# Hybrid trunk on one core: order of the second layer's input norms and first weights, low part of y on POOL, four banks for the q/k/v projection

## What is computed

```
for i in range(DEPTH):                       # 2 layers, x is (1, 512, 1024)
    hdn = rms_norm(x, norm_g[i])
    q, k, v, z (, f) = hdn @ w_in[i]         # 8 heads of 128, z a gate of the same width
    layer 0: q, k = rope(rms_norm(q)), rope(rms_norm(k)); y = causal block attention
    layer 1: q, k = rms_norm(q), rms_norm(k); y = attention with a bias from cumulated log f
    y = y * silu(z)
    x = x + y @ w_out[i]
```

## Time and profile before

| what | value |
| --- | --- |
| median of the runs | 556.06 us |
| the profiled execution | 555.65 us |
| its span, first to last instruction | 553.2 us |
| PE busy | 543.3 us, 98% |
| DVE busy | 408.5 us, 74% |
| POOL busy | 293.7 us, 53% |
| ACT busy | 286.9 us, 52% |
| granted TensorE clock, mean | 1.000 |

### The profile page before, as it was taken

How to read it: one execution, slowest core, us unless ns; L and a number is a source line. 1 busy time by engine, 2 the same in 40 slices (tenths; PEclk the granted TensorE clock), 3 DMA queues, 4 the chain that set the end, 5 groups by cost and what they waited for, 6 DMA issues and landing times.

```text
span 553.2 us, 9738 instructions
## 1 busy us (share of the span) xinstructions
PE 543.3 (98%) x2966; PEld 499.0 (90%) x2966; DVE 408.5 (74%) x1023; ACT 286.9 (52%) x841; POOL 293.7 (53%) x348
## 2 busy tenths in 40 slices
PE   6999999999999999999899999999999999999997
PEld 4999999999999999888688999999999999998887
DVE  3786899999999999974463767786868777779331
ACT  5746373737373737361445473837382837374400
POOL 5774545444444545451644486757565757476400
PEclk9999999999999999999999999999999999999999
DMA  9813313131313131222433336424241535132121
GB/s 259 244 22 111 103 54 100 55 98 57 95 57 95 57 95 57 95 78 73 108 95 78 96 80 95 99 74 105 67 118 53 118 53 133 53 118 70 45 95 58
DMA packets 78236, 49.94 MB, mean 90 GB/s; under 512 B 4089, under 2 KB 71417, under 8 KB 78210
## 3 DMA queue, kind: packets, MB, share of 16 engines
q1 hardware_dynamic: 78208, 49.61, 33.0%
q10 hardware_dynamic: 2, 0.00, 0.0%
HBM read 47.48 MB, written 2.11 MB: 90 GB/s over the span
## 4 chain that ended last, share of the span: by engine, by line
PE 50%; DVE 0%; issue 0%
PE banks L343 14%; PE banks L345 14%; PE banks L344 14%; PE banks L466 3%; PE banks L452 2%; PE banks L441 1%; PE banks L440 1%; PE banks L439 1%; PE banks L375 1%; PE banks L492 0%; PE banks L493 0%; DVE xs L948 0%; DVE xs L944 0%
## 5 line engine op out<-in xcount | busy, mean ns | idle before, releaser
L1079 POOL TENSOR_TENSOR w_lo<-w_raw,w_hi 128x512 fp32r<-128x512 f32 x147 | 190.1, 1306 | 82.9 <-ACT w_hi L602 82.9
L343 PE MATMUL banks<-w_hi,hT_hi 128*128 128x384 f32 x512 | 173.5, 339 | 2.6 <-DVE hT_lo L810 1.9
L344 PE MATMUL banks<-w_lo,hT_hi 128*128 128x384 f32 x512 | 171.6, 335 | 0.0
L345 PE MATMUL banks<-w_hi,hT_lo 128*128 128x384 f32 x512 | 171.6, 335 | 0.0
L867 DVE STREAM_TRANSPOSE banks<-qkn 32x256 f32<-32x256 f32 x240 | 109.4, 456 | 3.3
L343 PEld LDWEIGHTS banks<-w_hi,hT_hi 128*128 128x128 f32 x512 | 96.5, 188 | 4.5 <-POOL w_lo L1079 2.2
L344 PEld LDWEIGHTS banks<-w_lo,hT_hi 128*128 128x128 f32 x512 | 96.5, 188 | 0.6
L345 PEld LDWEIGHTS banks<-w_hi,hT_lo 128*128 128x128 f32 x512 | 96.4, 188 | 0.0
L602 ACT ACTIVATE w_hi<-w_raw 128x512 fp32r<-128x512 f32 x148 | 89.3, 638 | 13.5 <-DMA w_raw<-in_b_w_in_dram 13.4
L1095 POOL TENSOR_TENSOR msq<-ssq,eps 128x2 f32<-128x2 f32 x64 | 13.0, 203 | 127.1 <-ACT junk L638 127.1
L638 ACT ACTIVATE junk<-banks 128x128 bf16<-128x128 f32 x128 | 33.8, 271 | 48.8 <-PE banks L345 48.8
(11 more groups left out here) (110 smaller groups left out, 893.6 us busy)
## 6 DMA issues: line engine op xcount, KB each, us to landing
w_raw<-in_b_w_in_dram SPq DMA_DIRECT2D x64, 256.0 KB, 3.6
w_raw<-in_a_w_in_dram SPq DMA_DIRECT2D x52, 256.0 KB, 2.9
w_raw<-in_w_out_dram SPq DMA_DIRECT2D x32, 256.0 KB, 2.8
first_raw<-in_a_w_in_dram SPq DMA_DIRECT2D x12, 256.0 KB, 5.6
cos_t<-c_rows SPq DMA_DIRECT2D x8, 256.0 KB, 3.4
out_dram<-xs SPq DMA_DIRECT2D x7, 256.0 KB, 2.0
xs<-in_x_dram SPq DMA_DIRECT2D x3, 512.0 KB, 5.8
xs<-in_x_dram SPq DMA_DIRECT2D x2, 256.0 KB, 2.9
```

Source lines behind the costliest of these rows:

```text
L343: pe.matmul(dst, ah, bh, start=first and m == 0, stop=False)
L344: pe.matmul(dst, ah, bl, start=False, stop=False)
L345: mm = pe.matmul(dst, al, bh, start=False, stop=last and m == n - 1)
L1079: pool.tensor_tensor(w_lo[:, slot, k, :], raw, f32(w_hi[:, slot, k, :]), ALU.subtract).then_inc(wlo_set, by)
```

## The change

Four things. (1) The q/k/v projection of every head uses four banks, one for each tile (0, 1, 6, 7). The waits of PE (L393), ACT (L635) and POOL (L1094) that guard a reuse after two tiles now guard one after four, and the sums of squares and the reciprocal roots have four slots. The transposed q and k move to banks 4 and 5, which the transposed probabilities use as well, so that DVE's `turn_qk` gets one more wait, for the head's three low parts of probabilities. (2) In periods 1 to 6 of both layers the low part of y is made by POOL, between the reciprocal roots of tile 0 and the first weight chunk, and no longer by DVE ahead of the silu. (3) In the passage between the layers, on ACT the square of x tile t and the split of the transposed tile t - 1 stand ahead of the weight chunks 2t and 2t + 1 and no longer around them. (4) On POOL the reciprocal root of x tile t stands ahead of these two chunks.

```diff
-        ssq = sb("ssq", [P, 2, 2])
+        ssq = sb("ssq", [P, TILES, 2])
-        rstd = sb("rstd", [P, 2, 2])
+        rstd = sb("rstd", [P, TILES, 2])
-        Z_BANK, Y_BANK, QT_BANK, SPARE_BANK = 2, 3, 6, 6
+        Z_BANK, Y_BANK, QT_BANK, SPARE_BANK = 2, 3, 4, 6
         def qkv_bank(layer, h, t):
-            return (0, 1, 3, 4)[t] if layer == 0 and isinstance(h, int) and h == 0 else t % 2
+            return (0, 1, 3, 4)[t] if layer == 0 and isinstance(h, int) and h == 0 else (0, 1, 6, 7)[t]
         def turn_bank(layer, t):
-            return 3 if layer == 0 and t == 1 else QT_BANK
+            if layer == 1:
+                return QT_BANK
+            return 3 if t == 1 else SPARE_BANK
             def qkv(layer, h, slot, t):                       # PE
-                wait(pe, qkn_set, a - 1)
+                wait(pe, qkn_set, a - TILES + 1)
             def read_qkv(layer, h, s, t):                     # ACT
-                wait(act, rstd_set, a - 1)
+                wait(act, rstd_set, a - TILES + 1)
             def last(layer):                                  # ACT
                     for t in range(TILES):
-                        split_w(layer + 1, 0, 0, (2 * t, 2 * t + 1))
                         square_x(layer + 1, t)
                         if t >= 1:
                             split_hidden(layer + 1, t - 1)
+                        split_w(layer + 1, 0, 0, (2 * t, 2 * t + 1))
             def turn_qk(layer, h):                            # DVE
                 dve.wait_ge(qkn_set, TILES * (g + 1))
+                wait(dve, pTlo_set, 3 * g)
             def period(layer, h, s):                          # DVE
                 invert_sums(layer, h)
-                late_y(layer, h)
                 for n in range(4):
                     silu_part(layer, h, n)
             def last(layer):                                  # DVE
-                late_y(layer, h)
+                low_y(layer, h - 1)
             def rstd_qk(layer, h, t):                         # POOL
-                wait(pool, qkn_set, a - 1)
+                wait(pool, qkn_set, a - TILES + 1)
+            def low_y(layer, h):                              # POOL
+                g = HEADS * layer + h
+                pool.wait_ge(yhi_set, g + 1)
+                row = bass.ds(h, 1)
+                pool.tensor_tensor(yT_lo[:, row, :].rearrange("p a n -> p (a n)"), gz[:, 1, :],
+                                   f32(yT_hi[:, row, :].rearrange("p a n -> p (a n)")),
+                                   ALU.subtract).then_inc(ylo_set, 1)
             def period(layer, h, s):                          # POOL
                 rstd_qk(layer, h + 1, 0)
                 if layer == 1 and isinstance(h, int):
                     mask_bias(h)
+                if not isinstance(h, int):
+                    low_y(layer, h - 1)
                 split_w(layer, h + 2, s, (0,))
             def last(layer):                                  # POOL
                     for t in range(TILES):
+                        rstd_x(layer + 1, t)
                         split_w(layer + 1, 0, 0, (2 * t, 2 * t + 1))
-                        rstd_x(layer + 1, t)
```

More of the change, by code:

```diff
@@ L638, in read_qkv @@
                     sq = act.activation(junk[:, m, :], banks[:, qkv_bank(layer, h, t), m * P:(m + 1) * P],
-                                        ACT.Square, scale=SCALE, accum_out=ssq[:, t % 2, m:m + 1])
+                                        ACT.Square, scale=SCALE, accum_out=ssq[:, t, m:m + 1])
                 sq.then_inc(ssq_set, 1)
@@ L839, in norm_qk @@
                         last = dve.scalar_tensor_tensor(out=qkn[:, t, m, :], in0=banks[:, qkv_bank(layer, h, t), m * P:(m + 1) * P],
-                                                        scalar=rstd[:, t % 2, m:m + 1], in1=cos_t[:, 0, m, :],
+                                                        scalar=rstd[:, t, m:m + 1], in1=cos_t[:, 0, m, :],
                                                         op0=ALU.mult, op1=ALU.mult)
@@ L846, in norm_qk @@
                     dve.scalar_tensor_tensor(out=rot[:, t % 2, m].rearrange("p (a n) -> p a n", a=2), in0=swapped,
-                                             scalar=rstd[:, t % 2, m:m + 1],
+                                             scalar=rstd[:, t, m:m + 1],
                                              in1=sin_t[:, t, m].rearrange("p (a n) -> p a n", a=2),
@@ L852, in norm_qk @@
                     part = banks[:, qkv_bank(layer, h, t), m * P:(m + 1) * P]
-                    dve.scalar_tensor_tensor(out=part, in0=part, scalar=rstd[:, t % 2, m:m + 1], in1=cos_t[:, t, m],
+                    dve.scalar_tensor_tensor(out=part, in0=part, scalar=rstd[:, t, m:m + 1], in1=cos_t[:, t, m],
                                              op0=ALU.mult, op1=ALU.mult).then_inc(rot_set, 1)
@@ L1019, in begin @@
                 split_qk(layer, h)
-            def late_y(layer, h):
-                if not isinstance(h, int) or h > 0:
-                    low_y(layer, h - 1)
             def period(layer, h, s):
@@ L1093, in rstd_qk @@
                 pool.wait_ge(ssq_set, a + 1)
-                wait(pool, qkn_set, a - 1)
-                pool.tensor_tensor(msq[:, t % 2, :], ssq[:, t % 2, :], eps[:, :], ALU.add).then_inc(msq_set, 1)
+                wait(pool, qkn_set, a - TILES + 1)
+                pool.tensor_tensor(msq[:, t % 2, :], ssq[:, t, :], eps[:, :], ALU.add).then_inc(msq_set, 1)
                 pool.wait_ge(msq_set, a + 1)
-                pool.tensor_tensor(rstd[:, t % 2, :], msq[:, t % 2, :], power[:, :], ALU.pow).then_inc(rstd_set, 1)
+                pool.tensor_tensor(rstd[:, t, :], msq[:, t % 2, :], power[:, :], ALU.pow).then_inc(rstd_set, 1)
             pool.memset(one[:, :], 1.0).then_inc(ones_row, 1)
```

## The result

The changed kernel takes 563.4 us (median of 5 runs, 562.57 to 564.62) against 556.06; the ratio is 1.0134, with a 95% interval of 1.0119 to 1.015. That is slower, as forecast, by 7.3 us in place of 5.7, and the time lies 0.4 us above the upper end of the range. The profiled execution took 562.99 us; its span, 561.0, is 7.8 us longer than before.

What follows compares the result with a forecast made beforehand. PE, busy 98% of the span, was taken as the bound, with layer 0 paced by ACT, POOL and DVE. The sum 0.78 - 2.3 + 5.4 + 1.8 = +5.7 us gave 561.7 us, range 558.4 to 563.0.

Steps and rivals of the forecast that it cites:

- the ring of layer 0: Layer 0's period: ACT, POOL and DVE wait on each other in a round of 27.6 us, without PE.
- the own wait: DVE's added wait for its previous instruction before the block transposes: 0.13 us a round, six times, +0.78 us.
- a shorter layer 0: Rival: DVE's relief shortens layer 0 to 27.10 us a period, 558.5 us; chance 0.12.
- a slow POOL: Rival: POOL's low part of y takes 1.7 us, adding 0.4 us in six periods, 564.1 us; chance 0.10.
- weights in time: Rival: layer 1's weight chunks 6 and 7 come without a stall of PE, 554.5 us; chance 0.05.
- transposes of x tile 0 early: Passage between layers: PE's transposes follow unit (1,1) at once, next unit at 269.4 in place of 271.69, -2.3 us.
- stall before layer 1: PE waits at layer 1's first head for the low parts of weight chunks 6 and 7, +5.4 us.
- slow spell: After PE's standstill before layer 1, matmuls run at 1.2 GHz against 2.4 for some 3.7 us, +1.8 us.
- without them everything up to the transposes comes 2.5 us earlier: Passage: without two weight chunks ahead of x tile 0's square, work before PE's transposes moves up, covering the 2.3 us.
- needs 2.54 for two, up to 3.02: POOL's time for the low parts of weight chunks 6 and 7 before layer 1, starting at about 287.4.
- the start's rows: Near the kernel's start, after standing 1.85 us, PE's work took 3.73 us against 1.9 at full pace.
- the kept pace: PE stayed at full pace after pauses of about 1 us at 269; supported the full-pace rival, 559.9 us, chance 0.28.

Runs made afterwards that it cites:

- POOL aside: Kernel with chunk-by-chunk waits and both new orders, plus POOL's low parts of chunks 0 and 1 waiting for DVE's normalised x tile 0: 551.31 us, ratio 0.9913.
- filler in the stall: Changed kernel plus six unread float32 matmuls on PE ahead of layer 1's first tile: 560.28 us, ratio 1.0078.
- the loops alone: Changed kernel with the old ACT and POOL order in the passage between the layers: 556.44 us, ratio 1.0013.
- the added wait alone: Kernel before plus one wait in DVE's `turn_qk` for its own split of the probabilities: 556.92 us, ratio 1.0021.

## Why the prediction had the mechanism right and the size too small

The mechanism stood on each point. PE's transposes come early, the last two weight chunks come behind PE's last unit, PE stands and then runs at 1.2 GHz; the ring of layer 0 has no PE in it and got longer by the own wait. The rivals of a shorter layer 0, of a slow POOL and of weights in time are out. The time fell outside the range, by 0.4 us, because the terms were mis-sized, all in one direction. On the profiled executions:

| term | predicted | measured | from |
| --- | --- | --- | --- |
| layer 0's loop | +0.78 | +0.99 | values of period 0 to period 6: 165.88 against 164.89 |
| transposes of x tile 0 early | -2.3 | -1.7 | unit (1,2) starts at 271.55 and not 271.69, though all before it is 0.55 + 0.99 later |
| stall before layer 1 | +5.4 | +5.9 | 284.47 to 290.34 |
| slow spell | +1.8 | +1.95 | first tile to second: 7.32 against 5.37 |
| not predicted | 0 | +0.65 | 0.55 before the first values, 0.1 at the end |
| sum | +5.7 | +7.8 | |

Of the terms of the sum the largest misses, 0.6 in the second row and 0.5 in the third, have one cause: I priced DVE's and POOL's instructions as if they did not meet. The step "without them everything up to the transposes comes 2.5 us earlier", covering 2.3, moved DVE's normalising but let it keep its duration; in its new place POOL's low parts run beside both of its halves, and it takes 3.41 us, where it took 2.43 before. So PE waits 0.49 us for the second half (the line at L377 above), and from the first transpose to the next unit it is 1.51 us, not the 0.87 that I took. The experiment with POOL aside shows this one. In the stall the step "needs 2.54 for two, up to 3.02" took the lower end, and with DVE's normalising of x tile 3 beside them the two took 2.96; the start of the pair, 287.27, is where the chain put it, so 0.4 of the 0.5 us is that; the rest is mostly the 0.11 us from the low parts' end (290.23) to PE's start (290.34), which I had put at nothing. This second one is read from the trace and was not tested alone. For the two rows together I gave bounds of 2.9 and 3.6 us, and they measured 4.2: the upper bound had the slower low parts in it, but no smaller gain from the early transposes.

The slow spell was argued from the start's rows, and there from the pace alone: between 10.80 and 14.53 the profile shows a granted clock of 1.00, though the matmuls start 0.32 us apart. In the passage pace and granted clock agree: clock 0.50 after a stall of 5.87 us. With filler in the stall, and after a stall of 1.98 us, the clock stays at 1.00. The spell lasted 4.93 us and not 3.7, but with fifteen matmuls of 384 columns and no transposes in it, so the cost differed by only 0.15; that it came so close is partly luck. The prediction also named the Trainium skill (TensorE: Matmul & The Clock Gate, Part 1, What's actually happening): idle lowers the clock, sustained work raises it. The fall after the 5.87 us agrees with that.

One part of the argument did not hold. I took the kept pace after the two pauses of about 1 us at 269 as a sign that such pauses are harmless. In the trace with the low part of y on POOL, whose passage is that of the kernel before, the same two pauses are followed by a fall to 0.50 for 3 us (PE's timeline, then the stretch, columns as above):

```profile
270.35 0.66 PE L375 MATMUL banks<-ident,qkn 128*128 128x128 f32 x4 [1.02 <-DVE qkn L798]
272.02 1.12 PE L375 MATMUL banks<-ident,qkn 128*128 128x128 f32 x4 [1.01 <-DVE qkn L798]
...
272.02:275.07 3.05, 3.05 (x10) 2.57 (x10) 0.87 (x2) 2.58 (x6) 2.02 (x3) 0.50 0.46 108
```

It costs 1.5 us: from the second four transposes to those of x tile 1 (279.51) it is 7.49 us, against 5.98 in the kernel before. The traces of the kernel before, of the loops alone and of the added wait alone have nearly the same pauses, 0.74 to 1.05 us, and stay at 1.00. So these runs show that a stall of 5.9 us brought the low clock in both kernels that have it, and that two pauses of 1 us did so in one trace of four; what decides between them no run here shows.

In the loop the own wait was priced well: by itself it made the way from the values of period 0 to those of period 6 longer by 0.81 us, against the 0.78 of the sum; with the whole change it is 0.99. The 0.55 us ahead of the first values are not explained. 0.30 of them are there at PE's first projection (11.10 against 10.80), before anything that the change touches, and the first values come at 63.66 to 64.97 in the profiled executions of the other kernels, with the old banks as with the new.

## What to carry to other kernels

Before taking a wait off the busiest engine, follow the others once round the loop: if they close a ring as long as the period, only a link of the ring shortens it, and reordering one small instruction there can be worth more than removing 1.7 us beside it. When something is moved ahead of the last items of a list, ask who waits for the whole list. Price an instruction in its new place with its new neighbours. Before blaming a late load, look whether the engine behind it was free to use it.

## What was not expected of the hardware

Two-operand DVE and POOL instructions on SBUF hold each other up: the DVE pair 1.41 us alone, 2.42 beside part of POOL's pair and 3.41 beside all of it, while POOL's pair went from 2.53 to 2.96 and 2.99. DVE's splits of the transposed x, one of whose two inputs is in PSUM, took 1.27 us beside a POOL low part and 1.28 alone. A wait for the engine's own previous instruction moved DVE's next start from 0.09 us before the previous end to 0.03 us after it, and lengthened the period by 0.11 to 0.13 us when it was added alone.
